# Macaron decoder trunk with four mixers: the mixer's small matmuls regrouped, stick-breaking of four heads in wide operations, gate tanh in batches, FFN ends re-ordered

## The reference, cut to what matters

```python
h = x + 0.5 * swiglu(rms_norm(x, ffn1_norm), ffn1_w_in, ffn1_w_out)      # d_ff = 2816
u = rms_norm(h, mix_norm)
sb_qkv, s5_u, gq, gk, gv, gr, gg, dsa_qkv, gates = split(u @ w_in)      # gg has 16 columns only
y_sb  = stick_breaking_attention(sb_q, sb_k, sb_v)   # w = exp(logsig(z) + sum of logsig(-z) behind), strictly causal
y_s5  = s5_mixer(s5_u, ...)                          # complex diagonal scan over 1024 states, gelu, GLU
y_gla = gla_mixer(gq, gk, gv, gr, gg, w_gate, ...)   # z = gg @ w_gate + b_gate: decay of each key channel
y_dsa = dilated_mixer(dsa_q, dsa_k, dsa_v, ...)      # rms norm, rotary tables, three windows, softmax
mixed = sum over branches of sigmoid(gates) * (branch @ w_branch)
h = h + mixed @ w_out
h = h + 0.5 * swiglu(rms_norm(h, ffn2_norm), ffn2_w_in, ffn2_w_out)
```

## Time and profile before

| | |
|---|---|
| median of three runs | 1238.67 us (1238.65 to 1238.96) |
| the profiled execution | 1238.99 us, its span 1237.2 us |
| PE busy | 99% |
| DVE busy, ACT busy, POOL busy | 77%, 56%, 30% |
| granted PE clock | full in all 40 slices |
| DMA | 178 GB/s in the mean |

### The profile page before, as it was taken

One profiled execution on the slowest core, in us unless ns is written; L12 is line 12 of the kernel. 1 busy time (PEld: TensorE's weight loads), 2 busy tenths in 40 slices (PEclk: granted clock), 3 DMA queues, 4 the chain that ended last, 5 costly groups with the idle time before them and its releaser, 6 DMA issues.

```text
span 1237.2 us, 23636 instructions
## 1 busy us (share of the span) xinstructions
PE 1228.7 (99%) x9158; PEld 1151.8 (93%) x9158; DVE 946.9 (77%) x1244; ACT 689.9 (56%) x1021; POOL 367.8 (30%) x508
## 2 busy tenths in 40 slices
PE   9999999999999999999999999999999999999998
PEld 8999989999999999999999999999999999999998
DVE  6767788889887877666776778788997788766765
ACT  5666645773654565545566655558645445554553
POOL 0088990344404200000001889704443041000000
PEclk9999999999999999999999999999999999999999
DMA  8654454543344465455545454554333445555441
GB/s 311 238 202 159 182 182 177 186 139 135 137 164 174 174 239 203 176 179 194 174 167 205 175 198 173 188 183 171 137 136 137 170 172 205 182 192 192 169 181 69
DMA packets 32324, 220.44 MB, mean 178 GB/s; under 512 B 3712, under 2 KB 4352, under 8 KB 6272
## 3 DMA queue, kind: packets, MB, share of 16 engines
q1 hardware_dynamic: 31824, 218.96, 49.7%
q10 hardware_dynamic: 432, 0.52, 0.1%
HBM read 218.42 MB, written 1.05 MB: 177 GB/s over the span
## 4 chain that ended last, share of the span: by engine, by line
PE 93%; DVE 4%; ACT 1%; issue 1%; DMA 0%; POOL 0%; SPq 0%; DVEq 0%; ACTq 0%; POOLq 0%
PE banks L537 21%; PE banks L495 19%; PE banks L496 19%; PE banks L497 19%; PE banks L539 10%; PE banks L508 5%; DVE w_lo_t L1227 2%; ACT w_hi_t L900 1%; DVE hT L1459 1%; DVE u_t L1241 0%; DVE sbqk L1391 0%; DMA hT<-x_t 0%; DVE sbqk L1389 0%; PE banks L745 0%; DVE yb L1396 0%
## 5 line engine op out<-in xcount | busy, mean ns | idle before, releaser
L1227 DVE TENSOR_TENSOR w_lo_t<-raw,w_hi_t 128x1024 fp32r<-128x1024 f32 x398 | 505.6, 1310 | 97.8 <-ACT w_hi_t L900 97.4
L900 ACT ACTIVATE w_hi_t<-raw 128x1024 fp32r<-128x1024 f32 x398 | 397.3, 1046 | 116.1 <-PE banks L497 114.3
L495 PE MATMUL banks<-u_t,w_hi_t 128*128 128x256 f32 x944 | 271.8, 288 | 2.5 <-DVE u_t L1241 1.6
L496 PE MATMUL banks<-u_t,w_hi_t 128*128 128x256 f32 x944 | 266.9, 283 | 0.0
L497 PE MATMUL banks<-u_t,w_lo_t 128*128 128x256 f32 x944 | 266.8, 283 | 0.0
L537 PE MATMUL banks<-u_t,w_hi_t 128*128 128x512 f32 x576 | 204.0, 398 | 0.0
L537 PE MATMUL banks<-b_t,w_hi_t 128*128 128x512 f32 x576 | 204.0, 398 | 0.0
L495 PE MATMUL banks<-h_hi_t,w_hi_t 128*128 128x256 f32 x672 | 190.2, 283 | 0.4 <-issue 0.4
L496 PE MATMUL banks<-h_lo_t,w_hi_t 128*128 128x256 f32 x672 | 190.2, 283 | 0.0
L497 PE MATMUL banks<-h_hi_t,w_lo_t 128*128 128x256 f32 x672 | 190.1, 283 | 0.0
L495 PEld LDWEIGHTS banks<-u_t,w_hi_t 128*128 128x128 f32 x944 | 180.9, 192 | 9.7 <-issue 3.7
(11 more groups left out here) (246 smaller groups left out, 2011.0 us busy)
## 6 DMA issues: line engine op xcount, KB each, us to landing
raw<-weights SPq DMA_DIRECT2D x201, 1024.0 KB, 4.8
raw<-weights SPq DMA_DIRECT2D x3, 512.0 KB, 8.2
prm<-params SPq DMA_DIRECT2D x1, 1178.5 KB, 5.4
prm<-params SPq DMA_DIRECT2D x1, 1166.5 KB, 9.9
raw<-weights SPq DMA_DIRECT2D x4, 256.0 KB, 6.9
out_t<-hT SPq DMA_DIRECT2D x4, 256.0 KB, 2.4
cst<-constants SPq DMA_DIRECT2D x1, 896.0 KB, 10.3
hT<-x_t SPq DMA_DIRECT2D x1, 512.0 KB, 7.1
```

The source lines that it names most:

```text
L495: pe.matmul(o, st[0], mv[0], start=start, stop=False, skip_group_check=True)
L496: pe.matmul(o, st[0], mv[1], start=False, stop=False, skip_group_check=True)
L900: act.activation(w_hi[:, slot, a:a + HALF], raw[:, slot, a:a + HALF], ACT.Copy) \
L1227: dve.tensor_tensor(w_lo[:, slot, a:a + HALF], raw[:, slot, a:a + HALF], w_hi[:, slot, a:a + HALF].bitcast(F32), ALU.subtract) \
```

## The change

PE's pieces come in 10 groups of the mixer instead of 20 (12 with the two of the norm). Block `gg` leaves the stream: its 16 columns are computed by 8 plain float32 matmuls from `hT` (`gate_channels`, four column tiles of 32). Output tiles (4, 5) become two blocks of one tile. The S5 pairs 0 and 1 go through together; stick-breaking runs for four heads at once, with operations over two heads; masks touch only the 256 columns on the diagonal. Dilated weights go from DVE to ACT, and the tanh of five gates is done later, in batches. DVE at the end of an FFN does all residuals and splits first and the weights' rest after.

```diff
-SEQ = ["s5u", "sbq", "sbk", "gg", "gqk", "dq", "dk", (0, 0), "sbv", "gv", (0, 1), "dv", "gr", (1, 0), (1, 1),
+SEQ = ["s5u", "sbq", "sbk", "gqk", "dq", "dk", (0, 1), "sbv", "gv", (0, 0), "dv", "gr", (1, 0), (1, 1),
        (0, 2), (0, 3), (1, 2), (1, 3), (2, 0), (2, 1), (2, 2), (2, 3),
-OUT_TILES = [(0, 1), (2, 3), (4, 5), (6,), (7,)]
+OUT_TILES = [(0, 1), (2, 3), (4,), (5,), (6,), (7,)]
+TANH_AT = {m: [SEQ[m]] for m in range(NSEQ) if is_gate(m)}
+for later, earlier in [(12, (6, 9)), (17, (15, 16))]:
+    TANH_AT[later] = [SEQ[m] for m in earlier] + TANH_AT[later]
-SS_AFTER, ROW_AFTER = (4, 3, 4), 5
-S5_AT = (1, 5, 9, 13)
+SS_AFTER, ROW_AFTER = (4, 4, 4), 6
+S5_IN = {1: (0, 1), 3: (2,), 13: (3,)}
+S5_OUT = {11: 0, 18: 1}
@@ PE @@
-                    def s5_out(pair):
+                    def s5_out(half):
...
+                            for i in range(4 * half, 4 * half + 4):
+                    def gate_channels():
+                        pe.wait_ge(s.gg_w, layer * PER.gg_w + 1)
+                        for half in range(2):
+                            for j in range(4):
+                                kt = 4 * half + j
+                                a = PARAM["w_gg"][0] + 16 * kt
+                                ins = single(banks[32 * j:32 * j + 32, 2, T:2 * T], prm[:, a:a + 32], hT[:, kt, :],
+                                             half == 0, half == 1)
+                        ins.then_inc(s.gg, 1)
                     def pieces(m):
+                        if m == 1:
+                            gate_channels()
                         if m == 3:
-                            sb_scores(0), sb_scores(1)
-                        if m == 4:
-                            single(banks[:, 2, 0:T], p_("w_gate")[0:16, :], gq[0:16, :]).then_inc(s.gla_z, 1)
+                            sb_scores()
+                            for tt in range(2):
+                                ins = single(banks[:, 2 + tt, ATT:512], p_("w_gate"), gq[:, tt * P:(tt + 1) * P], False)
                         if m == 7:
-                            sb_suffix(0), sb_suffix(1)
+                            for h in range(HEADS):
+                                sb_suffix(h)
-                        if m == 12:
+                        if m == 11:
                             pe.wait_ge(s.sb_w, layer * PER.sb_w + HEADS)
                             attend(2, sbv, attA).then_inc(s.sb_o, 1)
-                            gla_scores(1)
-                        if m == 14:
+                            gla_scores()
+                        if m == 13:
                             attend(2, gv, attA).then_inc(s.gla_o, 1)
-                        if m == 16:
-                            dsa_scores(0), dsa_scores(1)
-                        if m == 17:
-                            dsa_scores(2), dsa_scores(3)
+                        if m == 15:
+                            dsa_scores()
                         if m == 19:
-                            dsa_turn(0), dsa_turn(1)
+                            for h in range(HEADS):
+                                dsa_turn(h)
@@ DVE, end of an FFN @@
                     residual(0)
-                    half_rest(layer, k0 + i + 1, 1, 0)
+                    residual(1)
                     split(0)
-                    residual(1)
-                    half_rest(layer, k0 + i + 1, 1, 1)
                     residual(2)
                     split(1)
                     residual(3)
                     split(2)
                     split(3)
+                    rest_of_weights(layer, k0 + i + 1, 1)
                     add_squares(layer * 3 + (1 if f == 0 else 3))
@@ DVE, pieces @@
-                    if m in (6, 9):
+                    if m in (5, 6):
+                        h = 0 if m == 5 else 2
+                        two = attA[:, h:h + 2, :]
+                        own.link(dve.scalar_tensor_tensor(out=two, in0=banks[:, SB_BANK[h]:SB_BANK[h] + 2, 0:ATT],
+                                                          scalar=0.0, in1=two, op0=ALU.max, op1=ALU.add))
+                        dve.tensor_tensor(diagonal(two), diagonal(two), strict, ALU.mult).then_inc(s.sb_sp, 1)
-                    if m in (8, 11):
-                        for h in (0, 1) if m == 8 else (2, 3):
-                            dve.scalar_tensor_tensor(out=attA[:, h, :], in0=attA[:, h, :], scalar=3e38,
-                                                     in1=c("strict"), op0=ALU.min, op1=ALU.mult)
                     if m == 10:
+                        for h in range(HEADS):
+                            one = attA[:, h, :].rearrange("p (c q) -> p c q", q=P)[:, 0:3:2, :]
+                            dve.scalar_tensor_tensor(out=one, in0=one, scalar=3e38, in1=strict[:, 0, :, :],
+                                                     op0=ALU.min, op1=ALU.mult).then_inc(s.sb_w, 1)
+                    if m == 9:
                         dve.wait_ge(s.gla_exp, layer * PER.gla_exp + 1)
...
-                    if m in S5_AT:
-                        s5_rotate(S5_AT.index(m))
-                    if m - 1 in S5_AT:
-                        s5_scan(S5_AT.index(m - 1))
+                    if m == 1:
+                        s5_times(0), s5_times(1)
+                    if m == 2:
+                        s5_add(0), s5_add(1)
+                    if m == 3:
+                        s5_scan(0), s5_scan(1)
+                    if m == 7:
+                        s5_times(2)
+                    if m == 8:
+                        s5_add(2), s5_scan(2)
+                    if m == 13:
+                        s5_times(3), s5_add(3)
+                    if m == 14:
+                        s5_scan(3)
@@ DVE, mixer @@
+                        if m == 19:
+                            for h in (1, 3):
+                                dve.wait_ge(s.dsa_pt, layer * PER.dsa_pt + h + 1)
+                                dve.tensor_copy(attB[:, h, :], banks[:, DSA_BANK[h], 0:ATT]).then_inc(s.dsa_pte_v, 1)
@@ DVE, start of layer 0 @@
-                    half_rest(0, 1, 0, 0)
                     norm_root(0)
-                    half_rest(0, 1, 0, 1)
+                    rest_of_weights(0, 1, 0)
                     norm_copy(0)
```

More of the change, by code:

```diff
@@ L185 @@
     dsa_s = HEADS
-    dsa_max = HEADS
+    dsa_max = 2
+    dsa_r = 2
+    rope_tab = 1
     dsa_exp = HEADS
@@ L199 @@
     m_lo = 8
-    dve = 54
-    act = 13
-    pool = 232
+    dve = 38
+    act = 9
+    pool = 236
 class Signals:
@@ L632, in ffn @@
                         in_block(b0 + 2, (b0 + 2) % 3, 6, where=f)
-                    in_block(b0 + 3, b0 % 3, 7, where=f)
+                    if layer == 0 and f == 0:
+                        for half in range(2):
+                            pe.wait_ge(s.w_lo, 4 * RING + half + 1)
+                            in_part(3, 0, 7, 0, range(4 * half, 4 * half + 4))
+                    else:
+                        in_block(b0 + 3, b0 % 3, 7, where=f)
                     pe.wait_ge(s.row_read, layer * PER.row_read + 2 * f + 1)
@@ L666, in attend, with s5_in @@
                         return ins
-                    def s5_in(pair):
+                    def s5_in(pairs):
+                        pair = pairs[0]
                         if pair == 0:
@@ L1174, in pieces, with dilated_weights @@
                         branch_hi(1, yb[:, 0, :, :].rearrange("p a t -> p (a t)"), 0.25)
+                def dilated_weights(h0):
+                    act.wait_ge(s.dsa_r, layer * PER.dsa_r + h0 // 2 + 1)
+                    for h in (h0, h0 + 1):
+                        act.activation(attB[:, h, 0:P], attB[:, h, 0:P], ACT.Copy, scale=dmx[:, h, 4:5])
+                        act.activation(attB[:, h, P:ATT], attB[:, h, P:ATT], ACT.Copy, scale=dmx[:, h, 5:6]) \
+                            .then_inc(s.dsa_p, 1)
                 def mixed_hi(dt):
@@ L1194, in mixer @@
                             continue
+                        if m == 17:
+                            dilated_weights(2)
+                        if m == 19:
+                            for h in (0, 2):
+                                act.wait_ge(s.dsa_pt, layer * PER.dsa_pt + h + 1)
+                                act.activation(attB[:, h, :], banks[:, DSA_BANK[h], 0:ATT], ACT.Copy) \
+                                    .then_inc(s.dsa_pte, 1)
                         round_weights(layer, k0 + m // RING + 1, m % RING)
-                        if is_gate(m):
-                            q, n = SEQ[m]
-                            act.wait_ge(s.evac_v, layer * PER.evac_v + NTH[m])
+                        for gate in TANH_AT.get(m, ()):
+                            q, n = gate
+                            act.wait_ge(s.evac_v, layer * PER.evac_v + NTH[SLOT[gate]])
                             x = G[:, n, 2 * q:2 * q + 2, :]
@@ new lines, in dilated_softmax @@
+                    bank = banks[:, DSA_BANK[h]:DSA_BANK[h] + 2, :]
```

(13 more changed lines are left out.)

396 lines of the change are left out of this document (208 added, 188 removed).

## The result

The changed kernel takes 1256.2 us (median, 1253.1 to 1257.5) against 1238.7: a ratio of 1.0138, interval 1.0125 to 1.0151. It is 17.6 us slower, where I had forecast 3 us faster, and it lies outside my range. The profiled execution has a span of 1255.7 us, before 1237.2.

The account below looks back on a forecast made before the run. The prediction took PE's issue time to bound the kernel. Against the profiled 1238.99 us, -15.2 (PE's work) - 1.5 (FFN ends) + 13.6 (new waits) = -3.1 gave 1235.9, as median 1235.6 us; range 1223 to 1242, chance 0.81.

Parts of the forecast that it names:

- PE's work: Mixer on PE: without gg and with fewer small groups, 7.6 us less a layer, 15.2 for both.
- Rival W: Four tiles don't run abreast in gate_channels, double s5_in and both s5_out: 6.9 us more, 1242.5 us; chance 0.08.
- FFN ends: DVE splits without weights between at the two mixer starts: net -1.5 us, bounds -2.5 to +0.5.
- the w_out blocks: Same matmuls, less rounding, no wait before: zero, bounds 0 to 1.
- The start of layer 0: Block 3's whole rounding now stands between the norm's root and its row: +0.25 us.
- New wait 1: PE waits at attend, m = 11, for sb_w from DVE: 5.0 us a layer, bounds 0 to 5.9.
- The kq step: DVE step ahead of attend's weights: 2.40 us alone, 4.05 with three steps colliding with POOL.
- New wait 2: PE waits at sb_suffix, m = 7, for masks of heads 2 and 3: 1.3 us a layer, bounds 0 to 2.0.
- New wait 3: PE waits for the GLU at m = 20: 0.5 us a layer, bounds 0 to 2.
- T + 16.8: End of New wait 1's chain without collisions, T being the end of block 8; PE comes at T + 17.3.
- rival S: Chains are full: waits of 9.9 us a layer, 19.8 in all, 1241.8 us; chance 0.10.
- Rival N: No new wait, POOL collides less than counted: 1222.0 us; chance 0.12.

Follow-up runs that it names:

- the last run: Changed kernel with pair 2's scans, masks, gelu and S5 chain reordered on DVE, old order at layer 0's start and second FFN end: 1224.1 us.
- POOL held: Changed kernel with one added wait: POOL begins S5's pair 2 only when attend's weights are done; 1236.3 us.
- ends alone: Kernel before with only DVE's new order at the FFN ends and layer 0's start, sum of squares not moved: 1242.6 us.

## Why the prediction was wrong, by its own steps

- **PE's work, -15.2: right, -14.4 measured.** In the last run the stretch from the end of block 1 to the end of the GLU group is 138.04 us in both layers; I said 137.6 without waits, before it was 145.2. Most groups met their row within 0.1 us; m = 3 is 3.31 (3.05 predicted). Rival W is wrong: m = 1 takes 2.08 us, not 3.7, so four tiles with 256 columns do run abreast.
- **FFN ends, -1.5: too good.** Alone they are worth 0.9 us, and in the two traces everything outside the two stretches is equal to 0.1 us (1237.2 - 2 x 145.23 before; after, 1255.7 - 155.25 - 153.79, the stretches from 212.03 to 367.28 and 834.61 to 988.40), so the w_out blocks and the rest, booked at 0, took the 0.9 us back; that last part was not tried by itself. The start of layer 0 was +0.27 as said.
- **New wait 1, 5.0 a layer: place and cause right, 5.67.** The experiment with POOL held confirms the 0.55 us for each collision. The kq step took 4.63 instead of 4.05 us because I counted three colliding steps in it and there are four: L1647, with one SBUF operand only, went from 0.28 to 0.83 us. The Trainium skill ("SBUF — State Buffer", Who interferes with whom) lists `tensor_scalar` among the operations that can take the pair shared with GpSimd; these two rows agree, and I had applied only its sentence on two inputs.
- **New wait 2, 1.3: it is 2.3,** over my upper bound of 2.0. I had taken a discount of 0.7 us for POOL's own pauses, and the chain was longer even than without it. DVE gets the weights of block 8 at 243.35, 2.4 us behind the end of block 5 and not 1.85, because ACT works on `attA` (L1147) until 241.6 before it takes that block out. The two collisions in the running sums, which cost 0.8 us together, I had booked at 0.85, though my own 0.55 each makes 1.1; with that the wait would have read 2.25. **New wait 3, 0.5: it is 1.75** (1.12 gelu, 0.63 copies), inside its bound; the copies' own wait was not in the sum. I had also ended the chain of wait 1 without collisions at T + 16.8, where its terms give 16.6; nothing hangs on it. Together 9.7 a layer instead of 6.8: 19.5 us for both, rival S almost to the number. S would have read 1242.
- **The missing term: the clock.** I priced a wait at its length. Group by group, behind the waits and against the last run at full clock, layer 0 lost 1.8 us at m = 7 and 4.7 + 0.9 at m = 11 and in the blocks behind it; layer 1 0.3, 4.7 and 0.9: 13.3 us. (The 0.3 stands at a clock of 1.00, so up to 0.3 us of each wait at m = 7 is something else than clock.) Nothing in my sum or in any rival had such a price; I read the granted clock of the kernel before (1.00 in all its slices) as a fact of the chip and not as something that PE's order of work can lose. The Trainium skill ("TensorE: Matmul & The Clock Gate", HAM oscillation — how this bites in real kernels) describes PE waiting for DMA long enough to be throttled again, so that what follows starts cold; this trace agrees for a wait on DVE, with 0.50 behind 5.67 us of idleness.

The sum by these measures: -14.4 + 0 + 19.5 + 13.3 = +18.4 us; the spans differ by 18.5. Without the losses behind the waits it would have been +5.1: already slower. So the step that failed is the size of the waits, booked at 6.8 us a layer and measured at 9.7, which alone turned the sign, and with it the missing price of the clock, which made the larger part of the distance. Rival N (1222.0) came true only in the last run, after DVE's and POOL's order had been repaired: the gain of the regrouping was real, and the waits stood before it.

## What to carry to other kernels

Shorter work on the busiest engine is worth nothing where another engine hands over just in time: first count that engine's strict order with its collisions, then move whatever releases the competitor behind the critical steps. Price a new wait of TensorE at its length, and a wait of 4 us or more also at the work behind it at half clock (2.3 us here with big matmuls behind it, 5.6 with a group of short ones); from 2.3 to 2.9 us on count this as a chance. If a wait can't be avoided, let big matmuls stand behind it, or fill it with matmuls that nobody reads: that gave back 9 us here, against 20 for removing the wait. A margin of zero on a chain of ten steps is to be booked at its upper bound.

## What the runs showed of the hardware

- After 4.2 and 5.7 us of idleness the granted clock was 0.50; after 2.3 us it was 0.50 in some layers and 1.00 in others, and with 2.9 us the mean clock of an execution was 0.992 to 0.997; with 1.4 us (ends alone) it was between 0.996 and 1.000; in the kernel before, whose longest wait after the start is 0.7 us, 0.999 to 1.000.
- At 0.50 the clock was back 4 us after the restart with big matmuls behind it, 12 us after it with 128 short ones first. In two of five profiled executions without a wait ahead of that group it fell at the group's end, in both layers.
- Two DVE and POOL instructions in conflict cost DVE 0.53 us a step whatever its size (four of 256 columns 1.42 to 3.54 us, two of 1024 columns 2.36 to 3.43), and a `tensor_scalar` with a single SBUF operand pays it too.
- Eight matmuls of 32 rows or 32 columns in four tiles and 256 columns each take about 1.0 us, as long as four in two tiles did.
